# The smaller expert's gate in two products, with silu and product behind the turn and the fold

## Chip, cores and metric

One core of a Trainium2 chip runs the whole program: two transformer-like blocks in one launch. The metric is the device time of that core in microseconds (us), as the median of several runs. The engines are TensorE (PE; its weight loads are listed as PEld), VectorE (DVE), ScalarE (ACT), GpSimd (POOL) and SyncE (SP), which issues the weight transfers.

## What is computed

The first block ends in a mixture of experts, which takes about half the time. Eight experts, the two best for each of 256 tokens:

```python
def swiglu(h, w_gate, w_up, w_down):
    return (jax.nn.silu(h @ w_gate) * (h @ w_up)) @ w_down

def moe_swiglu(h, w_router, w_gate, w_up, w_down):
    ...
    for e in range(N_EXPERTS):
        y = swiglu(h, w_gate[e], w_up[e], w_down[e])
        out = out + gates[..., e:e + 1].astype(h.dtype) * y
    return out
```

The width of the model is 1024, an expert's hidden width is 3584, everything is float32.

## The kernel before

**Pairs of experts.** The experts are sorted by how many tokens they got and go in four pairs: expert i = 0 of a pair has 128 slots for tokens, the smaller one, i = 1, has 64. `experts` is written once for each engine (ACT from L1185, DVE from L1838, PE from L2719) and runs once for each pair.

**Weights come in pieces.** A piece is 128 partitions x 2048 float32. A pair has PC = 84 pieces. SP loads each into one of NRX = 6 raw slots (L692). ACT rounds it to fp32r, the high part `wh` (L1150), DVE takes the difference as the low part `wl` (L1729), each into one of NW = 4 slots. So ACT may take up piece c+4 when PE has used piece c (semaphore `moe_used`), and SP may load piece c+6 when DVE has split piece c (`lo_moe`).

**Products.** The tokens are split as well, into `xhl` (high and low). With 128 slots a product of full precision takes three matmuls for each 512 columns (`mm3`, L2251 to L2253): high by high, high by low, low by high. The smaller expert's high and low tokens, 64 and 64, fit side by side into one stationary operand (`BOTH`), so two matmuls do (`mm2`, L2257 and L2258); the rows 0 to 63 of the result and the rows 64 to 127 have then to be added. Its up product and its down product go so, its gate product doesn't: there both halves of the 128 columns hold the same 64 tokens, and `mm3` gives the whole gate on 128 partitions.

**The steps of a pair.** The hidden width goes in NEJ = 4 steps j of 1024, 1024, 1024 and 512 (`STEPS`); a full step has four pieces of gate, four of up and four of down for each expert, the last one two each. PE's order in a full step j = 1, 2 is: gate(0,j), up(0,j), down(1,j-1), turned(0,j), gate(1,j), up(1,j), down(0,j), turned(1,j). `porder` is the order of the pieces. Step 0 has no down(1,.), and `slots_turned` in it. The last step ends with last_down(0), turned(1,3), the gathering of the next pair's tokens (L2708), last_down(1) and the scattering (L2821, L2822); the latter lies inside the next pair's first gate.

**Between up and down.** ACT takes silu of the gate out of PSUM into `esg` (L1202), DVE multiplies it with up into `eact` (L1873). `turned` then turns `eact` into columns of hidden units, by transposes for expert 0 (L2779) and by a product with the matrix `fold`, which turns and adds the two halves, for expert 1 (L2781). ACT rounds the result (`actT_hi`, L1189), DVE takes the rest (`actT_lo`, L1844), and the down product reads both. ACT and DVE do all of this in the order of their own loop over the pieces; `turn_behind` says at which piece they come to the rounding of the turned activations.

Of the kernel before, what the change touches and what calls it, by code (L numbers as in the profile page):

```python
# [16 lines left out]
def build(nc, IN, out):  # L17
# [43 lines left out]
    with ctx:  # L61
# [410 lines left out]
        for j in range(NEJ):  # L472
            if j:
                turn_behind[ppos[1, "d", j - 1, LASTK[j - 1]]] = (0, j)
            turn_behind[ppos[0, "d", j, LASTK[j]]] = (1, j)
# [118 lines left out]

        def gate_bank(i, j):

            return (6 if j == 0 else 2) if i else 0
# [5 lines left out]
        y_hi = [[acth[:, 0, :], acth[:, 1, :]], [eactTh[:, 4 * (1 - half):4 * (2 - half), :].rearrange("p k s -> p (k s)") for half in range(2)]]  # L603
# [338 lines left out]
        def _(act):  # L942
# [242 lines left out]
            def experts(at, more_follow):  # L1185

                def actT_hi(i, j):
                    act.wait_ge(sg("moe_Tfull"), at(2 * NEJ, 2 * j + i + 1))
                    V.activation(eactTh[:, 0:STEPS[j][1] // P, 0:CAP[i]], turned_act(i, j),  # L1189
                                 ACT.Copy).then_inc(sg("moe_actTh"), 1)  # L1190
# [194 lines left out]
        def _(dve):  # L1385
# [452 lines left out]
            def experts(at, more_follow):  # L1838

                def actT_lo(i, j):  # L1840
                    ks = slice(0, STEPS[j][1] // P)
                    low = eactTh[:, ks, CAP[1]:P] if i else eactTl[:, ks, :]
                    dve.wait_ge(sg("moe_actTh"), at(2 * NEJ, 2 * j + i + 1))
                    V.tensor_tensor(low, turned_act(i, j), eactTh[:, ks, 0:CAP[i]].bitcast(F32),  # L1844
                                    ALU.subtract).then_inc(sg("moe_actTl"), 1)

# [20 lines left out]
                for c, (i, kind, j, k) in enumerate(porder[:-2]):  # L1867
                    tail = kind == "d" and j == NEJ - 1
                    if kind == "u" and k == LASTK[j]:
                        width = STEPS[j][1]  # L1870
                        dve.wait_ge(sg("moe_used"), at(PC, c + 1))
                        dve.wait_ge(sg("moe_silu"), at(2 * NEJ, 2 * j + i + 1))
                        V.tensor_tensor(eact[:, 0:width], esg[:, 0:width], wide(up_bank(i, j), width),  # L1873
                                        ALU.mult).then_inc(sg("moe_act"), 1)
                    if c in turn_behind:
                        actT_lo(*turn_behind[c])
                    if tail:
                        y_low(0, k)
                    weights_lo(c)
# [323 lines left out]
        def _(pe):  # L2203
# [515 lines left out]
            def experts(at, more_follow, first=False, opening=False):  # L2719
# [8 lines left out]
                def gate_up(i, b0, kind, j, between=None):  # L2728
# [4 lines left out]
                    for q in range(KD // rows):  # L2733
# [38 lines left out]
                def turned(i, j):  # L2772

                    pe.wait_ge(sg("moe_act"), at(2 * NEJ, 2 * j + i + 2))
                    to = turned_act(i, j)
                    for k in range(STEPS[j][1] // P):
                        rows = eact[:, k // 2 * 256:(k // 2 + 1) * 256].rearrange("p (m two) -> p two m", two=2)[:, k % 2, :]
                        if i == 0:
                            ins = T.transpose(to[:, k, :], rows, ident[:, :])  # L2779
                        else:  # L2780
                            ins = T.matmul(to[:, k, :], rows, fold[:, :], start=True, stop=True)  # L2781
                    ins.then_inc(sg("moe_Tfull"), 1)
# [21 lines left out]
                def last_down(i):  # L2804

                    parts_ready(i, NEJ - 1)
                    for half in range(2):
                        hs = slice(half * 512, (half + 1) * 512)
                        for part in range(2):
                            h_, l_ = here(i, "d", NEJ - 1, part, 2)  # L2810
                            for k in range(2):
                                ins = down_part(i, bank[4 + 2 * i + half], 2 * part + k, h_[:, k, hs], l_[:, k, hs],
                                                False, part == 1 and k == 1)
# [49 lines left out]
                last_down(0)  # L2863
                turned(1, NEJ - 1)
# [242 lines left out]
```

## Time and profile before

| | us |
|---|---|
| median of three runs | 1715.86 (1714.61 to 1716.14) |
| the profiled execution | 1716.64 |
| its span, first to last instruction | 1714.9 |

The profiled execution shows a matmul busy for 98% of the span, DVE for 80%, ACT for 65%, and DMA at 400 GB/s and more in the part of the experts, which lasts from about 451 to about 1346 us. The granted TensorE clock is 0.995 of full speed over the span, so nearly always the level of 2.4 GHz. A busy matmul row counts the time from a matmul's start to its modelled end, and these overlap; the distance from start to start tells what one costs. DVE's and ACT's rows don't overlap in this way: idle time between them is idle time, but for some 0.1 us at the end of each instruction.

### The profile page before, as it was taken

Reading aid. Unit: us, or ns where it says so; the run is one execution under the profiler, and the core shown is the slowest. Engines: PE = TensorE matmul, PEld = TensorE weight load, DVE = VectorE, ACT = ScalarE, POOL = GpSimd, SP = SyncE. Lnnn points to the kernel's source line nnn. Section 1 sums busy time; section 2 is a strip of 40 time slices with the busy share of each in tenths; the row PEclk is TensorE's granted clock in tenths of the full one; section 3 lists DMA queues with packets and bytes.
Section 4 is the critical chain, followed back from the end, with each engine's and each line's share of the span. In section 5 each row is a group of like instructions: output and inputs, shape, how many; then the busy total and the mean of one; then the engine's idle time right before and its main releaser. Section 6 shows DMA issues by size and latency. Waiting matters only on the chain.

```text
span 1714.9 us, 24639 instructions
## 1 busy us (share of the span) xinstructions
PE 1686.8 (98%) x9514; PEld 1461.7 (85%) x9514; DVE 1374.2 (80%) x1099; ACT 1118.0 (65%) x911; POOL 145.2 (8%) x152
## 2 busy tenths in 40 slices
PE   9999999999989999999999999999999899999999
PEld 8879999898878888888888888888888798889998
DVE  7576454746889998999998999989999789778775
ACT  6445343464557888777887788777877655855553
POOL 7200000000010200000000000000000018500000
PEclk9999999999999999999999999999999999999999
DMA  7455655553479999999999999999999654326551
GB/s 255 169 149 193 201 173 195 172 178 143 163 294 390 411 408 406 362 384 414 402 408 367 378 407 408 403 363 394 395 410 403 241 167 134 113 99 221 176 194 50
DMA packets 181300, 479.76 MB, mean 280 GB/s; under 512 B 11807, under 2 KB 80185, under 8 KB 166857
## 3 DMA queue, kind: packets, MB, share of 16 engines
q1 hardware_dynamic: 180185, 476.43, 74.5%
q10 hardware_dynamic: 1008, 1.84, 0.3%
q8 instruction: 76, 1.25, 0.3%
q14 instruction: 31, 0.25, 0.0%
HBM read 477.18 MB, written 1.05 MB: 279 GB/s over the span
## 4 chain that ended last, share of the span: by engine, by line
PE 74%; DVE 10%; issue 5%; ACT 4%; DMA 4%; POOL 2%; DVEq 0%; ACTq 0%; SPq 0%; POOLq 0%
PE bank L2251 19%; PE bank L2253 19%; PE bank L2252 19%; DVE wl L1729 6%; DMA arena<-in_moe_w_down 3%; ACT wh L1150 2%; PE bank L2257 2%; PE bank L2258 2%; PE bank L2781 1%; PE bank L2370 1%; PE bank L2378 1%; PE bank L2371 1%; POOL arena L925 1%; POOL arena L924 1%; DMA raw<-in_moe_w_down 1%
## 5 line engine op out<-in xcount | busy, mean ns | idle before, releaser
L1729 DVE TENSOR_TENSOR wl<-raw,wh 128x2048 fp32r<-128x2048 f32 x224 | 508.8, 2299 | 54.1 <-ACT wh L1150 53.3
L1150 ACT ACTIVATE wh<-raw 128x2048 fp32r<-128x2048 f32 x224 | 426.8, 1918 | 108.7 <-PE bank L2253 80.4
L2251 PE MATMUL bank<-wh,xhl 128*128 128x512 f32 x768 | 303.5, 395 | 4.5 <-issue 4.5
L452 DVE TENSOR_TENSOR wl<-raw,wh 128x2048 fp32r<-128x2048 f32 x112 | 254.8, 2292 | 64.8 <-ACT wh L445 63.0
L2253 PE MATMUL bank<-wh,xhl 128*128 128x512 f32 x768 | 299.9, 391 | 0.0
L2252 PE MATMUL bank<-wl,xhl 128*128 128x512 f32 x768 | 299.7, 390 | 0.0
L2251 PE MATMUL bank<-xhl,wh 128*128 128x256 f32 x944 | 268.0, 284 | 0.2 <-DVE wl L452 0.2
L2253 PE MATMUL bank<-xhl,wl 128*128 128x256 f32 x944 | 267.1, 283 | 0.0
L2252 PE MATMUL bank<-xhl,wh 128*128 128x256 f32 x944 | 267.1, 283 | 0.0
L1729 DVE TENSOR_TENSOR wl<-arena,wh 128x2048 fp32r<-128x2048 f32 x112 | 256.9, 2308 | 8.9 <-ACT wh L1150 8.1
L445 ACT ACTIVATE wh<-raw 128x2048 fp32r<-128x2048 f32 x116 | 219.3, 1912 | 33.1 <-PE bank L2253 19.5
L1150 ACT ACTIVATE wh<-arena 128x2048 fp32r<-128x2048 f32 x112 | 213.6, 1914 | 35.6 <-PE bank L2253 18.7
L2251 PEld LDWEIGHTS bank<-xhl,wh 128*128 128x128 f32 x944 | 181.1, 192 | 2.1 <-issue 0.9
L2252 PEld LDWEIGHTS bank<-xhl,wh 128*128 128x128 f32 x944 | 181.1, 192 | 0.8
L2253 PEld LDWEIGHTS bank<-xhl,wl 128*128 128x128 f32 x944 | 181.1, 192 | 0.0
L2251 PEld LDWEIGHTS bank<-wh,xhl 128*128 128x128 f32 x768 | 144.9, 189 | 34.0 <-issue 4.6
L2253 PEld LDWEIGHTS bank<-wh,xhl 128*128 128x128 f32 x768 | 144.6, 188 | 30.7
L2252 PEld LDWEIGHTS bank<-wl,xhl 128*128 128x128 f32 x768 | 144.8, 189 | 29.2
L2251 PE MATMUL bank<-wh,arena_r 128*128 128x512 f32 x224 | 88.9, 397 | 3.6 <-DVE wl L1729 3.1
L2257 PE MATMUL bank<-wh,xhl 128*128 128x512 f32 x224 | 88.4, 395 | 0.0
L2258 PE MATMUL bank<-wl,arena_r 128*128 128x512 f32 x224 | 88.0, 393 | 0.0
L2257 PE MATMUL bank<-wh,arena_r 128*128 128x512 f32 x224 | 87.9, 392 | 0.0
(485 smaller groups left out, 2459.4 us busy)
## 6 DMA issues: line engine op xcount, KB each, us to landing
raw<-in_moe_w_up SPq DMA_DIRECT2D x96, 1024.0 KB, 7.9
raw<-in_moe_w_gate SPq DMA_DIRECT2D x64, 1024.0 KB, 7.8
raw<-in_moe_w_down SPq DMA_DIRECT2D x64, 1024.0 KB, 8.2
arena<-in_moe_w_gate SPq DMA_DIRECT2D x48, 1024.0 KB, 7.8
arena<-in_moe_w_down SPq DMA_DIRECT2D x48, 1024.0 KB, 8.1
raw<-in_w_up SPq DMA_DIRECT2D x22, 1024.0 KB, 5.3
arena<-in_moe_w_up SPq DMA_DIRECT2D x16, 1024.0 KB, 10.4
raw<-in_gla_w_in SPq DMA_DIRECT2D x12, 1024.0 KB, 7.2
```

The lines of the kernel that those rows point to most:

```text
L445: nc.scalar.activation(wh[:, i % NW, :], raw[:, i % NR, :], ACT.Copy).then_inc(hi_ready[ph], 1)
L452: V.tensor_tensor(wl[:, i % NW, :], raw[:, i % NR, :], wh[:, i % NW, :].bitcast(F32), ALU.subtract).then_inc(lo_of[i][0], 1)
L924: G(V.tensor_scalar(m["mt"][:, k:S], bz[:, b, 0:S - k], col("b_conv", 4 * (3 - k) + b), None, ALU.mult))
L925: G(V.tensor_tensor(bc[:, b, k:S], bc[:, b, k:S], m["mt"][:, k:S], ALU.add), "b_pre")
L1150: V.activation(wh[:, s, :], src, ACT.Copy).then_inc(sg("hi_moe"), 1)
L1729: V.tensor_tensor(wl[:, s, :], moe_raw(c)[0], wh[:, s, :].bitcast(F32), ALU.subtract).then_inc(lo_moe, 1)
L2251: T.matmul(o, xh, yh, start=first, stop=False)
L2252: T.matmul(o, xh, yl, start=False, stop=False)
L2253: return T.matmul(o, xl, yh, start=False, stop=last)
L2257: T.matmul(o, x, yh, start=first, stop=False)
L2258: return T.matmul(o, x, yl, start=False, stop=last)
L2370: T.matmul(ps[:, :], xh[:, kk, ts], h_[:, k, :], start=(kk == 0), stop=False)
```

## The change

The gate product of expert 1 takes two matmuls for each 512 columns like its up. Its two halves can't go into silu before they are added, so the order behind it changes: ACT copies the gate out of PSUM to `esg` and later the up to `eact` (four counts of `moe_silu` a step instead of two), `turned(1, j)` waits for both copies and multiplies both with `fold`, 16 products in a full step instead of 8. ACT takes silu of the turned gate (`folded_silu`), DVE multiplies it with the turned up (`folded_act`) into `eact`, and `actT_hi` and `actT_lo` read that instead of PSUM. These work on 512 columns in a full step (256 in the last). The rounding of expert 1 moves one piece later in ACT's and DVE's loops. In the last step `turned(1, 3)` moves from behind last_down(0) to between its two halves, and that step's turned activations use the upper half of their tile. The diff, without the changes to the slices of `y_hi`:

```diff
-            turn_behind[ppos[0, "d", j, LASTK[j]]] = (1, j)
+            turn_behind[ppos[0, "d", j, LASTK[j] if j < NEJ - 1 else 0]] = (1, j)
...
+        def folded(j, up):
+            n = STEPS[j][1] // P * CAP[1]
+            return wide(6 if j == 0 else 2, 2 * n)[:, up * n:(up + 1) * n]
...
+        NSG = 4 * NEJ
+        def first_chunk(i, j):
+            return 4 if (i, j) == (1, NEJ - 1) else 0
...
                 def actT_hi(i, j):
...
+                    if i == 0:
+                        act.wait_ge(sg("moe_Tfull"), at(2 * NEJ, 2 * j + 1))
+                        src = turned_act(i, j)
+                    else:
+                        act.wait_ge(sg("moe_act"), at(2 * NEJ, 2 * j + 3))
+                        src = by_chunk(eact[:, 0:n * CAP[1]])
...
+                def folded_silu(j):
+                    g = folded(j, 0)
+                    act.wait_ge(sg("moe_Tfull"), at(2 * NEJ, 2 * j + 2))
+                    V.activation(esg[:, 0:g.shape[1]], g, ACT.Silu).then_inc(sg("moe_silu"), 1)
...
-                        V.activation(esg[:, 0:width], wide(gate_bank(i, j), width), ACT.Silu).then_inc(sg("moe_silu"), 1)
-                    if c in turn_behind:
-                        actT_hi(*turn_behind[c])
+                        V.activation(esg[:, 0:width], wide(gate_bank(i, j), width),
+                                     ACT.Copy if i else ACT.Silu).then_inc(sg("moe_silu"), 1)
+                    if kind == "u" and k == LASTK[j] and i == 1:
+                        width = STEPS[j][1]
+                        act.wait_ge(sg("moe_used"), at(PC, c + 1))
+                        V.activation(eact[:, 0:width], wide(up_bank(i, j), width), ACT.Copy).then_inc(sg("moe_silu"), 1)
+                    ready = turn_behind.get(c, (None, 0))
+                    if ready[0] == 0:
+                        actT_hi(*ready)
+                    if turn_behind.get(c - 1, (0, 0))[0] == 1:
+                        actT_hi(*turn_behind[c - 1])
...
+                    if ready[0] == 1:
+                        folded_silu(ready[1])
...
+                def folded_act(j):
+                    u = folded(j, 1)
+                    n = u.shape[1]
+                    dve.wait_ge(sg("moe_silu"), at(NSG, 4 * j + 4))
+                    V.tensor_tensor(eact[:, 0:n], esg[:, 0:n], u, ALU.mult).then_inc(sg("moe_act"), 1)
...
-                    if kind == "u" and k == LASTK[j]:
+                    if kind == "u" and k == LASTK[j] and i == 0:
...
-                                if kind == "u" and i == 1:
+                                if i == 1:
...
+                        pe.wait_ge(sg("moe_silu"), at(NSG, 4 * j + 3))
+                        for src, to in ((esg, by_chunk(folded(j, 0))), (eact, by_chunk(folded(j, 1)))):
+                            for k in range(n):
+                                ins = T.matmul(to[:, k, :], rows(src, k), fold[:, :], start=True, stop=True)
...
-                last_down(0)
-                turned(1, NEJ - 1)
+                last_down(0, lambda: turned(1, NEJ - 1))
```

DVE's loop changes as ACT's does: `folded_act` stands where `folded_silu` stands, and `actT_lo` of expert 1 one piece later.

## Rows read from the trace of the kernel before

**Rows 1.** The page, part 1: busy time and share of the span.
```profile
PE 1686.8 (98%) x9514; PEld 1461.7 (85%) x9514; DVE 1374.2 (80%) x1099; ACT 1118.0 (65%) x911; POOL 145.2 (8%) x152
```
**Rows 2.** Busy time by stretch: PE, PEld, DVE, ACT, POOL; clock, DMA share, GB/s.
```profile
723.32:947.60 224.28, 223.78 (x1042) 186.00 (x1041) 207.81 (x113) 176.67 (x115) 0.00 (x0) 1.00 1.00 394
750.10:912.90 162.80, 162.31 (x754) 134.57 (x753) 150.70 (x78) 132.33 (x87) 0.00 (x0) 1.00 1.02 404
```
**Rows 3.** The page, part 6: a piece's transfer, its size and time to landing.
```profile
raw<-in_moe_w_up SPq DMA_DIRECT2D x96, 1024.0 KB, 7.9
```
**Rows 4.** Who waited for whom, 723.32 to 947.60: total us, times, longest.
```profile
PE bank L2251 <- DVE wl L1729: 0.4, 2, 0.2
ACT wh L1150 <- PE bank L2253: 26.3, 33, 3.5
DVE wl L1729 <- ACT wh L1150: 15.4, 22, 3.0
```
**Rows 5.** Timeline of PE, steps 1 and 2 of the second pair: start, us, line.
```profile
761.35 0.39 PE L2257 MATMUL bank<-wh,arena_r 128*128 128x512 f32 x1
...
788.26 0.47 PE L2251 MATMUL bank<-wh,arena_r 128*128 128x512 f32 x1 [0.19 <-DVE wl L1729]
...
799.27 2.00 PE L2781 MATMUL bank<-fold,arena 128*128 128x64 f32 x16
801.08 0.48 PE L2251 MATMUL bank<-wh,xhl 128*128 128x512 f32 x1
...
801.85 0.39 PE L2251 MATMUL bank<-wh,xhl 128*128 128x512 f32 x1
...
802.53 0.39 PE L2251 MATMUL bank<-wh,xhl 128*128 128x512 f32 x1
```
**Rows 6.** Timeline of DVE in step 1 of that pair: six of its rows.
```profile
762.99 1.22 DVE L1873 TENSOR_TENSOR arena<-arena,bank 128x1024 f32<-128x1024 f32 x1
764.12 6.69 DVE L1729 TENSOR_TENSOR wl<-raw,wh 128x2048 fp32r<-128x2048 f32 x3
770.73 2.28 DVE L1729 TENSOR_TENSOR wl<-arena,wh 128x2048 fp32r<-128x2048 f32 x1
772.93 1.22 DVE L1844 TENSOR_TENSOR arena_r<-bank,arena_r 128x1024 fp32r<-128x1024 f32 x1
...
783.62 2.29 DVE L1729 TENSOR_TENSOR wl<-raw,wh 128x2048 fp32r<-128x2048 f32 x1 [0.67 <-ACT wh L1150]
785.83 4.49 DVE L1729 TENSOR_TENSOR wl<-arena,wh 128x2048 fp32r<-128x2048 f32 x2
```
**Rows 7.** Busy time by stretch: step 1, step 0 and step 3.
```profile
762.99:788.12 25.13, 25.09 (x114) 20.34 (x112) 24.46 (x14) 21.82 (x14) 0.00 (x0) 1.00 1.01 406
...
707.97:726.73 18.76, 18.76 (x94) 15.88 (x93) 16.72 (x13) 15.22 (x11) 0.00 (x0) 1.00 1.00 398
870.92:891.95 21.03, 21.03 (x95) 17.18 (x93) 21.03 (x11) 17.84 (x11) 0.00 (x0) 1.00 1.04 405
```
**Rows 8.** Timeline of PE: step 0 of that pair, then step 3.
```profile
706.33 0.39 PE L2251 MATMUL bank<-wh,xhl 128*128 128x512 f32 x1
...
726.73 0.39 PE L2251 MATMUL bank<-wh,arena_r 128*128 128x512 f32 x1
...
892.08 0.50 PE L2251 MATMUL bank<-wh,arena_r 128*128 128x512 f32 x1
...
896.31 1.05 PE L2781 MATMUL bank<-fold,arena 128*128 128x64 f32 x8
897.17 0.36 PE L2708 MATMUL bank<-arena_r,xnh 128*128 128x256 f32 x1
```
**Rows 9.** Timeline of ACT behind them: the copies of the gathered tokens.
```profile
898.25 4.03 ACT L1214 ACTIVATE xhl<-bank 128x512 fp32r<-128x512 f32 x8
```
**Rows 10.** The first pair: its step 0 on PE, and a stretch around it.
```profile
460.00:500.00 40.00, 35.52 (x174) 30.02 (x173) 31.49 (x29) 25.44 (x18) 5.86 (x3) 0.91 0.79 294
...
477.66 0.77 PE L2251 MATMUL bank<-wh,xhl 128*128 128x512 f32 x1 [4.47 <-issue]
```
**Rows 11.** Duration min/median/max in ns, of two groups: silu and rounding on ACT.
```profile
L1202 ACT ACTIVATE arena<-bank x32: 577/1029/1034, 459.3 to 1335.7; 128x1024 f32<-128x1024 f32 x24, 128x512 f32<-128x512 f32 x8
L1189 ACT ACTIVATE arena_r<-bank x32: 383/598/1031, 491.9 to 1345.9; 128x512 fp32r<-128x512 f32 x16, 128x1024 fp32r<-128x1024 f32 x12, 128x256 fp32r<-128x256 f32 x4
```

More of the change, by code:

```diff
@@ L601, in up_bank @@
             return (2 if j == 0 else 0) if i else 2
-        y_hi = [[acth[:, 0, :], acth[:, 1, :]], [eactTh[:, 4 * (1 - half):4 * (2 - half), :].rearrange("p k s -> p (k s)") for half in range(2)]]
+        y_hi = [[acth[:, 0, :], acth[:, 1, :]], [eactTh[:, 4 * half:4 * (half + 1), :].rearrange("p k s -> p (k s)") for half in range(2)]]
         y_lo = [[actl[:, 0, :], actl[:, 1, :]], [eactTl[:, 4 * half:4 * (half + 1), :].rearrange("p k s -> p (k s)") for half in range(2)]]
@@ L1840, in actT_lo @@
                 def actT_lo(i, j):
-                    ks = slice(0, STEPS[j][1] // P)
-                    low = eactTh[:, ks, CAP[1]:P] if i else eactTl[:, ks, :]
+                    n = STEPS[j][1] // P
+                    k0 = first_chunk(i, j)
+                    low = eactTh[:, k0:k0 + n, CAP[1]:P] if i else eactTl[:, 0:n, :]
+                    src = by_chunk(eact[:, 0:n * CAP[1]]) if i else turned_act(i, j)
                     dve.wait_ge(sg("moe_actTh"), at(2 * NEJ, 2 * j + i + 1))
-                    V.tensor_tensor(low, turned_act(i, j), eactTh[:, ks, 0:CAP[i]].bitcast(F32),
+                    V.tensor_tensor(low, src, eactTh[:, k0:k0 + n, 0:CAP[i]].bitcast(F32),
                                     ALU.subtract).then_inc(sg("moe_actTl"), 1)
+                def folded_act(j):
[3 more added lines that the diff above has]
+                    V.tensor_tensor(eact[:, 0:n], esg[:, 0:n], u, ALU.mult).then_inc(sg("moe_act"), 1)
                 def weights_lo(c):
@@ L2772, in turned, with rows @@
                 def turned(i, j):
[L2774 to L2781, printed above, removed]
+                    def rows(src, k):
+                        return src[:, k // 2 * 256:(k // 2 + 1) * 256].rearrange("p (m two) -> p two m", two=2)[:, k % 2, :]
+                    n = STEPS[j][1] // P
+                    if i == 0:
+                        pe.wait_ge(sg("moe_act"), at(2 * NEJ, 2 * j + 2))
+                        to = turned_act(i, j)
+                        for k in range(n):
+                            ins = T.transpose(to[:, k, :], rows(eact, k), ident[:, :])
+                    else:
+                        pe.wait_ge(sg("moe_silu"), at(NSG, 4 * j + 3))
+                        for src, to in ((esg, by_chunk(folded(j, 0))), (eact, by_chunk(folded(j, 1)))):
+                            for k in range(n):
+                                ins = T.matmul(to[:, k, :], rows(src, k), fold[:, :], start=True, stop=True)
                     ins.then_inc(sg("moe_Tfull"), 1)
@@ L2802, in down, with last_down @@
                         used(ins)
-                def last_down(i):
+                def last_down(i, between=None):
                     parts_ready(i, NEJ - 1)
                     for half in range(2):
+                        if half and between is not None:
+                            between()
                         hs = slice(half * 512, (half + 1) * 512)
@@ L2811, in last_down @@
                             for k in range(2):
-                                ins = down_part(i, bank[4 + 2 * i + half], 2 * part + k, h_[:, k, hs], l_[:, k, hs],
-                                                False, part == 1 and k == 1)
+                                ins = down_part(i, bank[4 + 2 * i + half], first_chunk(i, NEJ - 1) + 2 * part + k,
+                                                h_[:, k, hs], l_[:, k, hs], False, part == 1 and k == 1)
                             if half:
```

19 lines of the change are left out of this document (13 added, 6 removed).

## The prediction, made before the changed kernel was run

> **What bounds the kernel now.** I read the busy shares first. A matmul is busy for 98% of the span, DVE for 80% [rows 1], and in one whole pair of experts, 224.28 us long, PE is busy for 223.78 us and DVE for 207.81 us [rows 2]. That looks like a kernel bound by TensorE, from which every removed matmul comes off. The waits of the same pair say the same at first sight: PE waits for a split weight for 0.4 us in all, while ACT waits 26.3 us for PE to free a slot [rows 4].
>
> Next I read how the two engines run against each other inside a step. A matmul of 512 columns costs 0.227 us from start to start (801.85 to 802.53 for three) [rows 5]. So a piece that goes through three products holds PE for 12 x 0.227 = 2.72 us, and one that goes through two for 8 x 0.227 = 1.81 us. DVE takes 2.21 us for the split of a piece (three in 6.69 us, less the overlap at their ends: 764.12 to 770.73) [rows 6]. PE is therefore slower than DVE on three-product pieces and faster on two-product pieces. Only four split slots lie between them. In each full step there is a stretch that starts when up of expert 0 is done and ends at the start of down(0,j): down(1,j-1), the transposes, gate(1,j) and up(1,j). In step 1 it runs from 761.35 to 788.26, 26.91 us [rows 5], and ends with PE waiting 0.19 us for a split by DVE [rows 5]. Over that stretch, from the end of the last split that belongs to the slow part, DVE is busy for 24.46 of 25.13 us; its one gap is 0.67 us [rows 6, 7]. The reader is to see this: PE and DVE have the same length there, and PE only looks alone at the bound.
>
> Last the transfers. Between 750.1 and 912.9 the DMA share is 1.02 at 404 GB/s [rows 2]. A piece is 1024 KB, 1.049 MB [rows 3], so one lands every 2.59 us at that rate, and 84 need 218 us. The pair takes 224.3 us, so DMA alone would leave 6 us a pair.
>
> One rule of the Trainium skill speaks against this change. The page "Perfetto Trace Analysis", section "Identifying the Most-Contended Engine", says that matmul busy time is no measure of TensorE's headroom, that the busy share of its weight loads is to be used, and that the engine with the highest occupancy is to be optimized first. Here the weight loads are at 186.00 of 224.28 us, 83%, and DVE at 93% [rows 2]: by the rule DVE is the one to relieve, and the rows of the stretch agree. By the matmul row the sum would be the first rival's, by the rule about nothing is gained where DVE is full.
>
> **What is removed.** gate(1,j) loses one matmul of three. A pair has 7 blocks of 512 columns x 8 blocks of rows = 56 of them, 56 x 0.227 = 12.7 us of PE's time: 3.63 us in each full step, 1.82 us in the last. On DVE the product of 1024 columns (1.22 us [rows 6]) becomes one of 512, but it stood and stands outside the stretch.
>
> **What is added on PE.** A fold of a full step, 8 products (16 matmul rows), takes 1.81 us, from 799.27 to 801.08 [rows 5]; the last step's half takes 0.86 us, 896.31 to 897.17 [rows 8]. The change does twice as many: +1.81 us in each of three steps, +0.86 in the last, 6.3 us a pair. They lie in the slow part, where nothing else sets PE's pace, so they are paid in full. So PE's own work falls by 12.7 - 6.3 = 6.4 us a pair.
>
> **What the removed matmuls are worth, step by step.** Steps 1 and 2: the stretch can shrink only until DVE's chain is without a gap, since mult and rounding of expert 0 and the splits of all its pieces stay as they are. The gap is 0.67 us. With gate(1,j) at 1.81 us a piece PE will wait for splits several times in gate(1,j) and up(1,j), some 3 us in all. So -0.67 +1.81 = +1.14 us each. Step 0: the stretch is gate(1,0), transposes, slots, up(1,0), from 706.33 to 726.73 [rows 8]. DVE is busy in it for 16.72 of 18.76 us [rows 7], so it can shrink by 2.04 us; -2.04 +1.81 = -0.2 us. Step 3: DVE has no gap, 21.03 of 21.03 us [rows 7]; PE starts the second down piece at 892.08, right at the end of that chain [rows 8]. Nothing is gained, and the fold costs 0.86 us. That it stands between the halves now doesn't make it free: no split is late there that PE would otherwise wait for.
>
> **Copies and moved waits.** ACT gets copies of gate and up, 1.03 us each in a full step by silu's row [rows 11]. The gate's copy stands where silu stood. The up's copy is behind up(1,j), and turned(1,j), which waits for it, comes 10.9 us later in PE's order (four slow pieces), 2.7 us in the last step (one half of last_down). If that cover were gone it would cost 0.9 us a step; its place is then ahead of the split of piece c+4, which PE wants three pieces later. folded_silu and folded_act (512 columns, about 0.6 us by the rows of rounding at that size [rows 11]) hold the next split on ACT and DVE until PE has folded, as the rounding does today; the pause grows by 1.8 us. What waits behind it is the split of the next gate's fourth piece, which PE wants 8.2 us after the fold: I count it as hidden. At the end of the pair ACT's chain is longer by silu, and by the rounding, which is now behind one more split of 1.9 us. The copies of the gathered tokens start today 1.08 us behind PE's first gathering product (898.25 against 897.17) [rows 8, 9]. I add 0.3 us for them: between 0, if the earlier fold makes up for it, and 1.9 us, a whole split.
>
> **The sum.** Second and third pair: -0.2 + 2 x 1.14 + 0.86 + 0.3 = +3.2 us each. The first pair differs: its step 0 comes behind a pause of 4.47 us, and DVE is busy for only 31.49 of the 40 us around it [rows 10], so the whole 3.63 us and about 1 us of a wait behind it should come off: -4.6 + 1.8 + 2.3 + 1.2 = +0.7. In the last pair there is no gathering, but the scattering waits for low parts that stand behind the same chain; I take the same end: +3.2. Together +10.3 us, taken as +10: 1716.64 + 10 for an execution such as the profiled one, 1715.86 + 10 = **1725.9 us** for the median, which lies 0.8 us below the profiled time.
>
> Bounds of the unknown terms: if DVE's chain also loosens at its start, a stretch may win some 0.9 us more in each of the 8 middle steps and 1.6 us in each of three first ones (all of 3.63): -12 us. If none of the gaps can be used: 8 x 0.67 + 3 x 2.04 = +11 us, rarely all of it, and with the 1.9 us at the pairs' ends +6. That gives about 1714 to 1742 as outer ends and 1719 to 1733 as the forecast's own range.
>
> **Rivals.** *TensorE bound (faster).* PE's busy time is right, splits and transfers follow. Then 4 x 6.4 = 25.6 us come off: 1690. For it speaks that PE hardly waits in the whole pair [rows 4]; against it the 24.46 of 25.13 us [rows 7]. It decides if ACT and DVE can be 3 us ahead at the start of a stretch, for which there are only four slots. Chance 0.10. *Half of it.* The transfers allow 6 us a pair but DVE gives way in part, say by 3 us a pair: 1703. Chance 0.08. On what the transfers allow there is a page, "DMA: Bandwidth & Descriptors" of the Trainium skill, section "Bandwidth", which gives 425 GB/s for large transfers: by that a pair would need an estimated 207 us and not 218. The rows show 404 at a share above 1, and either figure leaves this rival open. *A draw.* Step 0 and the first pair give what steps 1 to 3 take: within 3.4 us of 1716. Chance 0.14. *The forecast*, slower by some 10 us by the full DVE chain: 0.56. *Transfers run dry (slower still).* The longer pause of DVE at the fold lets no raw slot free for about 6 us, the queue empties after step 0, and in the next stretch PE waits for data as well as for splits: at 2.59 us a piece a hole of one piece in two steps of each pair is 4 x 2 x 2.59 = 21 us, half of it on top of the forecast's waits: 1736. It decides if fewer than three transfers are under way at a fold; today a piece takes 7.9 us to land [rows 3], three pieces' time. Chance 0.12. That the change doesn't remove the matmuls is no rival: their number follows from the loops.
>
> **Numbers.** Faster by over 0.2%, which is about what a measurement of this kernel can tell from no change (3.4 us): 0.18. Within it: 0.14 and 0.03 from the near end of the forecast, 0.17. Slower: 0.53 + 0.12 = 0.65. The range that should hold 8 in 10 leaves out the first rival and parts of the second and of the last: 1707 to 1736.
>
> **What would show it.** Right: mm3 on xhl falls by 224 matmuls in each of three rows, mm2 grows by 224 in each of two, fold rows go from 224 to 448. In step 1 of the second pair the stretch to down(0,1) stays above 26 us with PE waiting some 3 us for DVE's splits, DVE has no gap in it, and two folds take 3.6 us; a pair takes about 227.5 us. PE's waits on DVE grow from 0.4 us to 7 or more a pair. Wrong: the pair is shorter than 224 us, or a stretch is shorter than 26 us (then the start of DVE's chain isn't where I put it), or ACT waits for transfers at each stretch's end (then the last rival).

## The result, and the profile after

The changed kernel takes 1728.6 us (median of 4, 1727.2 to 1729.7) against 1715.7 us (median of 4, 1714.6 to 1716.1): 1.0079 times the time before, 95% interval 1.0066 to 1.0091. It is slower by 13 us, where 10 us were forecast. The profiled execution has a span of 1726.9 us at a granted clock of 0.996.

First the page of the changed kernel, parts 1 and 5: busy time and share of the span; then a group's busy time, the mean ns of one, and the idle time ahead of it.

```profile
PE 1679.0 (97%) x9514; PEld 1440.9 (83%) x9514; DVE 1366.4 (79%) x1099; ACT 1135.7 (66%) x943; POOL 145.8 (8%) x152
...
L2300 PE MATMUL bank<-wh,xhl 128*128 128x512 f32 x544 | 214.4, 394 | 0.0
...
L2306 PE MATMUL bank<-wh,xhl 128*128 128x512 f32 x448 | 183.7, 410 | 18.8 <-DVE wl L1765 10.9
```

The change did what it says. The three-product rows went from 768 matmuls to 544, the two-product rows from 224 to 448. (The number of all PE instructions is the same by chance: 224 matmuls fewer, 112 folds of two records more.) PE is busy for 7.8 us less than in [rows 1], and the span is 12 us longer. The last row already says why: the two-product matmuls stood behind 18.8 us of idle time, 10.9 of them for splits by DVE.

Now three stretches of the second pair, to be held against [rows 2, 7]: a whole pair, step 1's stretch from down(1,0) to down(0,1), and step 0's stretch from gate(1,0) to down(0,0). They start at PE's first matmul of the stretch; those of [rows 7] start up to 1.6 us later in it. Columns: PE, PEld, DVE, ACT and POOL busy; clock, DMA share, GB/s.

```profile
726.88:954.78 227.90, 221.88 (x1041) 180.89 (x1040) 206.20 (x113) 181.19 (x122) 0.00 (x0) 1.00 0.99 387
764.51:791.04 26.53, 24.41 (x105) 18.40 (x104) 26.19 (x13) 22.39 (x13) 0.00 (x0) 1.00 1.01 391
709.92:727.26 17.34, 17.16 (x85) 14.00 (x84) 17.34 (x12) 16.89 (x11) 0.00 (x0) 1.00 1.01 414
```

In step 0's stretch DVE is busy for 17.34 of 17.34 us, and in step 1's for 26.19 of 26.53. With the same bounds DVE was busy for 26.24 of 26.91 us (step 1) and 18.36 of 20.40 (step 0) before. PE, which had 0.18 us of idle time in step 1's stretch before and none in step 0's, now has 2.12 and 0.18. The waits of that pair, to be held against [rows 4] (total us, times, longest):

```profile
ACT wh L1165 <- PE bank L2302: 19.3, 20, 3.5
...
PEld bank L2306 <- DVE wl L1765: 7.3, 10, 1.6
...
PE bank L2306 <- DVE wl L1765: 3.1, 5, 1.2
...
PE bank L2300 <- DVE wl L1765: 1.5, 5, 0.5
```

PE's weight loads of the two-product matmuls now wait 7.3 us a pair for DVE's splits, all its weight loads 9.0 us, where it was 1.3 before (the matmul of the piece waits on top of a load that waits, so the two rows overlap and aren't to be added). ACT waits less for PE, 19.3 us for 26.3.

The timeline of PE through step 1 of the second pair shows where (start, us, line; in brackets the idle time ahead and who ended it):

```profile
742.65 0.48 PE L2300 MATMUL bank<-wh,xhl 128*128 128x512 f32 x1
...
764.51 0.39 PE L2306 MATMUL bank<-wh,arena_r 128*128 128x512 f32 x1
...
779.56 0.50 PE L2306 MATMUL bank<-wh,xhl 128*128 128x512 f32 x1 [1.18 <-DVE wl L1765]
...
781.86 0.47 PE L2306 MATMUL bank<-wh,xhl 128*128 128x512 f32 x1 [0.17 <-DVE wl L1765]
...
788.65 0.50 PE L2306 MATMUL bank<-wh,xhl 128*128 128x512 f32 x1 [0.36 <-DVE wl L1765]
...
791.04 0.47 PE L2300 MATMUL bank<-wh,arena_r 128*128 128x512 f32 x1 [0.28 <-DVE wl L1765]
...
802.01 3.89 PE L2836 MATMUL bank<-fold,arena 128*128 128x64 f32 x32
805.71 0.48 PE L2300 MATMUL bank<-wh,xhl 128*128 128x512 f32 x1
```

The stretch is 791.04 - 764.51 = 26.53 us where it was 26.91: of the 3.63 us of removed matmuls 0.38 us are left. Behind it stands a fold of 805.71 - 802.01 = 3.70 us in place of 1.81. The step is 63.06 us, before 61.59.

The second pair piece by piece, each from the starts of PE's first and last matmul in the timeline:

| second pair | before, us | after, us | difference | forecast |
|---|---|---|---|---|
| step 0 (gate(0,0) second half, to gate(0,1)) | 49.48 | 49.05 | -0.43 | -0.2 |
| step 1 | 61.59 | 63.06 | +1.47 | +1.14 |
| step 2 | 61.59 | 62.70 | +1.11 | +1.14 |
| step 3, gathering, scattering | 51.48 | 53.09 | +1.61 | +1.16 |
| pair | 224.14 | 227.90 | +3.76 | +3.2 |

### The profile page after: what moved, and what is told of

Same layout as the page of the kernel before. It is cut to its first block, busy times and chain, and to the rows that moved or that the text cites. A ratio compares the mean times of both kernels' runs of the same rounds, so it can differ in the third digit from the quotient of the medians.

```text
span 1726.9 us, 24720 instructions
## 1 busy us (share of the span) xinstructions
PE 1679.0 (97%) x9514; PEld 1440.9 (83%) x9514; DVE 1366.4 (79%) x1099; ACT 1135.7 (66%) x943; POOL 145.8 (8%) x152
## 3 DMA queue, kind: packets, MB, share of 16 engines
HBM read 477.18 MB, written 1.05 MB: 277 GB/s over the span
## 4 chain that ended last, share of the span: by engine, by line
PE 66%; DVE 17%; issue 9%; ACT 4%; POOL 2%; DMA 1%; DVEq 0%; ACTq 0%; POOLq 0%; SPq 0%
PE bank L2300 17%; PE bank L2302 17%; PE bank L2301 17%; DVE wl L1765 11%; PE bank L2836 3%; ACT wh L1165 2%; DVE arena_r L1882 1%; PE bank L2419 1%; PE bank L2427 1%; PE bank L2420 1%; POOL arena L940 1%; POOL arena L939 1%; DMA arena<-in_moe_w_down 1%; DVE arena L1917 1%; PE bank L2306 1%
## 5 line engine op out<-in xcount | busy, mean ns | idle before, releaser
L1165 ACT ACTIVATE wh<-arena 128x2048 fp32r<-128x2048 f32 x112 | 214.1, 1915 | 38.8 <-PE bank L2302 19.9
L2300 PE MATMUL bank<-wh,xhl 128*128 128x512 f32 x544 | 214.4, 394 | 0.0
L2301 PE MATMUL bank<-wl,xhl 128*128 128x512 f32 x544 | 211.8, 389 | 0.0
L2302 PE MATMUL bank<-wh,xhl 128*128 128x512 f32 x544 | 211.8, 389 | 0.0
L2306 PE MATMUL bank<-wh,xhl 128*128 128x512 f32 x448 | 183.7, 410 | 18.8 <-DVE wl L1765 10.9
L2307 PE MATMUL bank<-wl,xhl 128*128 128x512 f32 x448 | 176.7, 394 | 0.0
L2301 PEld LDWEIGHTS bank<-wl,xhl 128*128 128x128 f32 x544 | 102.2, 188 | 20.4
L2307 PEld LDWEIGHTS bank<-wl,xhl 128*128 128x128 f32 x448 | 85.0, 190 | 16.0
```

Of the source, the lines that this page charges most:

```text
L1165: V.activation(wh[:, s, :], src, ACT.Copy).then_inc(sg("hi_moe"), 1)
L2300: T.matmul(o, xh, yh, start=first, stop=False)
L2301: T.matmul(o, xh, yl, start=False, stop=False)
L2302: return T.matmul(o, xl, yh, start=False, stop=last)
L2306: T.matmul(o, x, yh, start=first, stop=False)
L2307: return T.matmul(o, x, yl, start=False, stop=last)
```

## The experiments

The theory is that of the prediction: removed matmuls are worth only what DVE's chain in the stretch leaves (0.67 us in a full step, 2.04 in step 0), and the added folds are paid in full. The rivals are TensorE as the bound, the transfers running dry, and a loss that comes from the copies or the moved waits.

**One part alone: the two products without the rest.** e1 is the kernel before with this edit:

```
-    if kind == "u" and i == 1:
+    if i == 1:
         ins = mm2(b, x[:, kk, BOTH], h_[:, kk % rows, ns], l_[:, kk % rows, ns], kk == 0, kk == KD - 1)
```

> The kernel before, with the gate product of expert 1 in two matmuls and nothing else changed: the addition of its two halves ahead of silu is left out, so part of the computation is missing. It shows what the removed matmuls are worth by themselves. Theory (DVE's chain of splits ends the stretch from up(0,j) to down(0,j)): 0.7 us in each full step, 2 to 3 us in step 0, about 3.7 us a pair, 15 us in all: 1701. Rival, TensorE alone is the bound: 224 x 0.227 = 51 us, 1665. Rival, the transfers give the rest: 6 us a pair, 1691.

Measured: 1705.6 us (1704.5 to 1706.8), 0.9947 of before (0.9931 to 0.9962). Its busy time by stretch, down(1,0) to down(0,1), and PE's waits in it:

```profile
757.58:783.73 26.15, 24.34 (x106) 18.40 (x104) 26.15 (x14) 23.47 (x14) 0.00 (x0) 1.00 1.00 399
```
```profile
772.63 0.50 PE L2257 MATMUL bank<-wh,xhl 128*128 128x512 f32 x1 [1.19 <-DVE wl L1729]
774.92 0.47 PE L2257 MATMUL bank<-wh,xhl 128*128 128x512 f32 x1 [0.19 <-DVE wl L1729]
783.73 0.47 PE L2251 MATMUL bank<-wh,arena_r 128*128 128x512 f32 x1 [0.18 <-DVE wl L1729]
```

DVE is busy for the whole 26.15 us, and PE waits for it three times, the first time for the same 1.2 us as in the changed kernel. So copies and moved waits are not what makes PE wait: without any of them a full step wins 0.78 us (61.59 to 60.81) of 3.63. TensorE as the bound would have given 4 x 12.7 = 51 us for this edit; 9 came. That is less than the 15 expected. Step 0 and the full steps of the second pair came as expected (-2.23 and -0.78 us), but its step 3, where DVE had no gap, grew from 51.48 to 51.93 us, with waits of 0.37 and 0.70 us for splits in down(0,3), and step 0 of the first pair won 1.80 us.

**The added part alone: the folds twice.** e2 is the kernel before, and `turned(1, j)` does its folds a second time into a bank that nobody reads:

```
         else:
+            T.matmul(to[:, k, :], rows, fold[:, :], start=True, stop=True)
+    if i == 1:
+        n = STEPS[j][1] // P
+        to = bank[7 if j == 0 else 3][:, 0:n * CAP[1]].rearrange("p (k s) -> p k s", k=n)
+        for k in range(n):
+            rows = eact[:, k // 2 * 256:(k // 2 + 1) * 256].rearrange("p (m two) -> p two m", two=2)[:, k % 2, :]
             ins = T.matmul(to[:, k, :], rows, fold[:, :], start=True, stop=True)
```

> The kernel before, with each fold of expert 1 done a second time into a free bank: only the added products. Theory: they lie where PE alone sets the pace and are paid in full, 1.9 us in each full step and 0.9 us in the last, 6.6 us a pair, +26 us: 1742. Rival, they hide under a wait: 1716 to 1720. Together with the first run this should give the change: -15 + 26 = +11 us.

Measured: 1739.7 us (1738.4 to 1740.3), 1.0144 (1.0129 to 1.0160): +25.0 us, 6.2 us a pair. The second set of folds starts 1.83 us behind the first:

```profile
743.21 2.00 PE L2781 MATMUL bank<-fold,arena 128*128 128x64 f32 x16
...
745.04 2.06 PE L2787 MATMUL bank<-fold,arena 128*128 128x64 f32 x16
```

The folds are paid in full, four pairs times 6.3 us. e1 and e2 together give -9.1 + 25.0 = +15.9 us; the change as a whole gives +13. Each of the three differences is known to some 2 to 3 us, so the 3 us between them may be noise.

**The change in step 0 alone.** e5 makes every edit of the change conditional on (i, j) = (1, 0); steps 1 to 3 stay as before. The core of it:

```
-    if i == 1:
+    if i == 1 and (kind == "u" or j == 0):
         ins = mm2(...)
```

> The change in step 0 of each pair alone; steps 1 to 3 as before. In the trace of the changed kernel step 0 of the second pair is 0.4 us shorter than before, in the first pair it is as long as before. Theory: -0.4 us in three pairs, 1.2 us in all, 1714.5, not to be told from no change. Rival, TensorE bound: (3.63 - 1.89) x 4 = 7 us, 1709.

Measured: 1713.6 us (median of 11, 1711.2 to 1715.6), 0.9991 (0.9982 to 1.0000). In the second pair step 0 takes 739.11 - 690.06 = 49.05 us, the 0.43 us less of the table, and steps 1 and 2 take 61.59 and 61.56 us as before. Step 0 is a draw, and it lends nothing to or from its neighbours. The 13 us of loss are in steps 1 to 3.

**DVE relieved.** e3 (on the kernel before) and e4 (on the changed kernel) do half of the low parts of an expert's weights. What is left out: the other 1024 columns of each split keep what stood in the slot.

```
-    V.tensor_tensor(wl[:, s, :], moe_raw(c)[0], wh[:, s, :].bitcast(F32), ALU.subtract).then_inc(lo_moe, 1)
+    V.tensor_tensor(wl[:, s, 0:1024], moe_raw(c)[0][:, 0:1024], wh[:, s, 0:1024].bitcast(F32), ALU.subtract).then_inc(lo_moe, 1)
```

> The kernel before, with DVE taking the low part of only half the columns of each expert's piece (half of the low parts is left out): a split takes about 1.2 us instead of 2.3. Theory: PE hardly waits for DVE in the kernel before, so it gains only the 0.2 to 1 us waits at the stretches' ends, 1 us a pair: 1711, at most 6 us. Rival, DVE is the bound of the kernel before as a whole: more than 10 us.

> The changed kernel with the same relief of DVE (half of the low parts left out). Theory: PE no longer waits in the long stretch; a pair falls from 227.9 to about 218 us, where PE's own work (217 us) and the transfers (218 us) lie: 1728 - 38 = 1690, so that against the relieved kernel before the change gains some 20 us. Rival, the copies, the later rounding or the new waits are what costs: 1715 or more.

Measured: e3 1698.6 us (1697.6 to 1699.4), 0.9901 (0.9885 to 0.9918); e4 1696.8 us (1696.1 to 1698.3), 0.9892 (0.9876 to 0.9909). For e4 the rival (copies, rounding and new waits cost the time: 1715 or more) falls: with DVE relieved the changed kernel is 32 us shorter. But 38 us were expected, and a lead of some 20 us over the relieved kernel before; it is 1.7 us ahead of e3, where it was 13 us behind the kernel before. What holds e4 comes with the transfers, below. For e3 the expectation misses too. At most 6 us were expected of a kernel that I took to be limited by DVE almost nowhere; 16.5 us came. The busy time by stretch of e3, and the same up(1,1) as in [rows 5]:

```profile
716.00:938.00 222.00, 221.94 (x1040) 186.06 (x1039) 122.88 (x112) 175.98 (x114) 0.00 (x0) 1.00 1.01 397
```
```profile
769.12 0.39 PE L2257 MATMUL bank<-wh,xhl 128*128 128x512 f32 x1
...
776.38 0.39 PE L2251 MATMUL bank<-wh,arena_r 128*128 128x512 f32 x1
```

up(1,1) takes 7.26 us, as 32 x 0.227 must; before it took 7.78 (780.48 to 788.26), of which the trace calls 0.19 a wait on DVE. The whole step falls from 61.59 to 60.94 us. The larger part, 9.0 us, is at the first pair. PE reaches it 2.7 us earlier (458.57 to 455.88), and its step 0 falls from 55.95 to 49.62 us: 2.7 of that ahead of gate(1,0), where PE's pause shrinks from 4.47 to 1.79 us, 2.1 in the stretch and 1.5 in down(0,0) (a wait of 0.99 us among it). Not all of it is waiting: the 2.1 us in the stretch are the clock's, as PE's first matmuls of gate(1,0) show, before and then in e3 (the last columns: clock, DMA share, GB/s):

```profile
477.66:482.06 4.40, 4.40 (x10) 3.45 (x11) 1.19 (x2) 0.63 (x1) 0.00 (x0) 0.50 0.84 356
```
```profile
472.28:476.70 4.42, 4.42 (x19) 3.64 (x20) 1.19 (x2) 1.96 (x2) 0.00 (x0) 1.00 1.03 422
```

Behind the long pause the granted clock was 0.50, the level of 1.2 GHz, and 10 matmuls took the time in which e3, behind the short one, did 19 at 1.00: gate(1,0) took 13.07 us before and 11.01 in e3. So DVE cost the kernel before some 16 us, part of it through the clock behind PE's pauses. This matters for the one term of the sum that was badly sized (below).

The Trainium skill ("Perfetto Trace Analysis", section "Identifying the Most-Contended Engine") says to judge TensorE by its weight loads, and to optimize the engine with the highest occupancy first. The runs agree: weight loads are 186 of 224 us, DVE 208, and halving DVE's low parts gave 16.5 us where removing 12.7 us of matmuls a pair (e1) gave 9.

**Transfers.** e7 is the changed kernel with half of each piece transferred (the split reads the whole slot, and the other half of it is left from earlier), e8 is e4 with the same, e9 is e3 with the same:

```
-    sp.dma_start(to.rearrange("p (k n) -> p k n", k=src.shape[1]), src).then_inc(arrived, 16)
+    kh = src.shape[1] // 2
+    sp.dma_start(to.rearrange("p (k n) -> p k n", k=2 * kh)[:, 0:kh, :], src[:, 0:kh, :]).then_inc(arrived, 16)
```

> The changed kernel with half of each expert piece transferred (the other half of each raw slot is left as it was, so half of the weights is missing). Theory: DVE's chain still ends the stretches, so 0 to 4 us at the places where ACT waits for transfers today: 1724 to 1728. Rival, the transfers run dry: a fall to 1715 or below.

> The changed kernel with both, half the split and half the transfer (half of the weights and of their low parts left out). Theory: now PE's own work is the bound, about 217 to 218 us a pair, 4 x 6.1 us under the kernel before treated the same way, which should stand at about 1710: 1686. If ACT's chain (1.8 us a piece, 12 pieces and two more instructions in a long stretch) is next, up to 1 us a step more: 1694.

> The kernel before with half the split and half the transfer (half of the expert weights and of their low parts left out), to be set against the changed kernel treated the same way (1676.6). Theory: with DVE relieved PE never waited in the kernel before, so the transfers give nothing more: 1697 to 1699, and the change then gains about 22 us, near the 25 us that its matmuls and folds make on PE. Rival, the transfers held the relieved kernel before too: 1690 or below, and the change gains 10 us or less.

Measured: e7 1728.9 us, 1.0078 (1.0061 to 1.0094), the time of the changed kernel; e8 1676.6 us, 0.9774 (0.9758 to 0.9791); e9 1698.3 us, 0.9900 (0.9885 to 0.9915), the time of e3. The rival of transfers running dry falls with e7: half the bytes, and nothing comes back. But e8 is 20 us below e4, more than forecast. e4 and e8 by stretch, one pair each:

```profile
710.00:932.00 222.00, 219.28 (x1048) 183.24 (x1048) 122.86 (x116) 182.04 (x124) 0.00 (x0) 1.00 1.01 400
```
```profile
710.00:927.00 217.00, 216.42 (x1042) 182.60 (x1041) 121.61 (x113) 178.96 (x122) 0.00 (x0) 1.00 0.67 204
```

A pair of e4 takes 221.8 us (a third of the way from the first to the last of the four copies of the slots' table; before it is 225.0 by the same mark), and 84 pieces of 1.049 MB at its 400 GB/s take 220: behind DVE stand the transfers, some 3 us a pair below the time before. Once both are out of the way a pair takes 216.9 us, and PE is busy for 216.42 of 217. A full step is then 59.20 us against e9's and e3's 60.94: -1.74, which is -3.63 + 1.89. e8 minus e9 is -21.6 us. That is what the change is worth where TensorE is the bound, close to the first rival's 25.6. The rival's arithmetic was right, and its condition wasn't met.

On the DMA's limit the Trainium skill ("DMA: Bandwidth & Descriptors", section "Bandwidth") has 425 GB/s for a transfer of 16 MB, and 341 for one of 1 MB, the size of this kernel's pieces. By the first a pair would need an estimated 207 us and e4 would not have been held; the second is below what every trace here shows. The traces have 387 to 400 GB/s over whole pairs at a share of about 1.0 (394 before, so it is not 400 and more throughout, as "Time and profile before" has it), and up to 417 in a short stretch (e11, below); e4 was held, and the measurement decides.

**The fast pieces moved apart.** If DVE is late only because two-product pieces stand together, another order should help. e6 is the changed kernel with the pieces of a full step in another order (the list, PE's program and the waits alike):

```
-    g(0,j) u(0,j) d(1,j-1) t(0,j) g(1,j) u(1,j) d(0,j)
+    g(0,j) d(1,j-1) u(0,j) g(1,j) t(0,j) u(1,j) d(0,j)
```

> The changed kernel with another order of the pieces in steps 1 to 3: gate(0,j), down(1,j-1), up(0,j), gate(1,j), turned(0,j), up(1,j), down(0,j), turned(1,j). So never more than eight two-product pieces follow one another, as in step 0, where twelve did. PE's and DVE's work is the same. Theory (what costs is the length of the stretch, against four split slots): PE waits 3 us less in each full step, 220 to 221 us a pair against 227.9 us, near the 218 us that the transfers need: 1701, between 1695 and 1708. Rival, DVE or the transfers as a whole are the bound: no better than 1724.

Measured: 1725.2 us (1722.0 to 1728.9), 1.0063 (1.0046 to 1.0079). This misses by 24 us. A full step takes 62.06 us. The order brought a wait of its own, of PE for ACT's copy of the gate:

```profile
777.55 1.10 PE L2832 MATMUL bank<-ident,arena 128*128 128x128 f32 x8
779.94 0.50 PE L2307 MATMUL bank<-wh,xhl 128*128 128x512 f32 x1 [1.29 <-ACT arena L1229]
```

Since 24 pieces at 2.59 us are also 62.2 us, the transfers could be blamed. e12 is e6 with e7's edit, half of each piece transferred:

> The kernel with the fast pieces apart (1725.2 us), and of every piece of an expert's weights only the first half is transferred; the split reads the whole slot as before, and the second half of it is what an earlier transfer left there. Open is what holds its full steps at 62.06 us. Transfers' theory: PE's own work of such a step is 12 x 2.72 + 12 x 1.81 + 0.86 + 3.70 = 58.9 us, its waits for the gate's copy and for DVE add 1.7 us, 60.6; the rest to 62.06 (24 pieces at 2.59 us are 62.2) is the transfers'. With half of them a full step takes 60.6 us, a pair 4 to 5 us less, and the kernel about 1708. Rival: the transfers are only as long as the step is, as with the changed kernel (halving them there gave nothing, 1728.9 against 1728.6), and DVE and the copies set the step: 62 us a step, within 3 us of 1725.

Measured: 1722.2 us (1721.5 to 1723.0), 1.0037 (1.0025 to 1.0050). The transfers give 3 to 4 us, not 17; a full step still takes 62.08 us, although the wait for the gate's copy has fallen from 1.29 to 0.26 us. In its place PE waits 0.88 us for a split. Busy time by stretch, then DVE's timeline:

```profile
757.04:790.13 33.09, 31.68 (x139) 24.89 (x138) 33.09 (x17) 29.36 (x18) 0.00 (x0) 1.00 0.71 210
770.40:788.16 17.76, 16.44 (x73) 12.73 (x72) 17.76 (x10) 16.66 (x11) 0.00 (x0) 1.00 0.69 210
```
```profile
754.83 2.29 DVE L1767 TENSOR_TENSOR wl<-raw,wh 128x2048 fp32r<-128x2048 f32 x1 [1.33 <-ACT wh L1167]
757.04 4.49 DVE L1767 TENSOR_TENSOR wl<-arena,wh 128x2048 fp32r<-128x2048 f32 x2
761.45 8.89 DVE L1767 TENSOR_TENSOR wl<-raw,wh 128x2048 fp32r<-128x2048 f32 x4
770.25 2.29 DVE L1767 TENSOR_TENSOR wl<-arena,wh 128x2048 fp32r<-128x2048 f32 x1
```

DVE works without a gap through 33 us, and through the whole of gate(1,1) and up(1,1). Those eight fast pieces (14.5 us on PE) still stand together, against eight splits and now both the product and the rounding of expert 0 (8 x 2.21 + 2 x 1.13 = 19.9 us of DVE, from which only the lead that four slots allow can be taken off). Parting down(1,j-1) from them was the wrong cut; that wasn't tried further.

**The gate's fold moved into the stretch.** If a stretch is set by DVE, PE's work put into it should be free, and behind it it is paid. In the changed kernel both folds stand behind down(0,j). e10 does the gate's fold in the middle of up(1,j):

```
+    def folded_gate(j):
+        pe.wait_ge(sg("moe_silu"), at(NSG, 4 * j + 2))
+        for k in range(STEPS[j][1] // P):
+            T.matmul(by_chunk(folded(j, 0))[:, k, :], rows(esg, k), fold[:, :], start=True, stop=True)
...
-    gate_up(i, up_bank(i, j), "u", j)
+    gate_up(i, up_bank(i, j), "u", j, (lambda: folded_gate(j)) if i else None)
```

> The changed kernel with one move on TensorE: the 8 folds of the gate (4 in the last step) are issued in the middle of up(1,j), inside the stretch in which PE waits for DVE's splits anyway, and only the 8 folds of the up stay behind down(0,j). Theory: in a full step PE waits about 3 us there, so 1.9 us of folds vanish in the wait: full steps of 63.1 and 62.7 us become 61 us, step 0 gains about 0.8 us and step 3 about 0.6 us, a pair falls from 227.9 to 222.8 us, in all 1728 - 20 = 1708, below the kernel before. Rival, the folds delay the release of split slots and so DVE by their own length: 1724 or more. Rival, the transfers hold a full step at 62 us: 1721.

Measured: 1710.9 us (median of 8, 1709.1 to 1712.5), 0.9975 (0.9965 to 0.9986). Against the kernel before, step 0 of the second pair wins 1.77 us, full steps 0.1 us, and step 3 still loses 0.70. The moved fold isn't quite free: of its 1.85 us (half of 3.70) the full steps get back 1.57 and 1.18 us and step 0 gets back 1.34, and the stretch of step 1 grows from 26.53 to 26.94 us. So e11 does this in step 0 alone and leaves steps 1 to 3 as they were, which is e5 with e10's edit:

> The change in step 0 alone (steps 1 to 3 as in the kernel before), and in it the fold of the gate's copy stands in the middle of up(1,0), where PE runs at 1.81 us a piece and DVE sets the pace, and not beside the fold of the up's copy behind down(0,0). Theory (a product put into the stretch costs nothing as long as DVE is behind, one behind the stretch costs in full): moving the gate's fold took step 0 of the second pair from -0.43 us against the kernel before to -1.77 us when it was done in all four steps. The run with the change in step 0 alone took 1713.6 us; 4 x 1.34 us come off it: about 1708, 0.4% below the kernel before, and steps 1 and 2 of the second pair keep 61.6 us each. Rival (the 1.77 us of step 0 are lent by the next step: DVE is as late there and gives it back): no better than the run with the moved fold in all steps, about 1711, and step 1 of the second pair is above 62 us.

Measured: 1708.3 us (1706.7 to 1709.1), 0.9955 (0.9942 to 0.9969): faster than both kernels, by 7.7 us and by 20. Busy time of its step 0's stretch, then PE's timeline through step 0:

```profile
705.29:723.99 18.70, 18.70 (x102) 16.15 (x100) 18.41 (x14) 16.91 (x11) 0.00 (x0) 1.00 1.02 417
```
```profile
688.97 0.39 PE L2308 MATMUL bank<-wh,xhl 128*128 128x512 f32 x1
...
718.45 2.00 PE L2835 MATMUL bank<-fold,arena 128*128 128x64 f32 x16
720.26 0.48 PE L2314 MATMUL bank<-wh,xhl 128*128 128x512 f32 x1
...
723.99 0.39 PE L2308 MATMUL bank<-wh,arena_r 128*128 128x512 f32 x1
...
734.87 2.00 PE L2853 MATMUL bank<-fold,arena 128*128 128x64 f32 x16
736.68 0.48 PE L2308 MATMUL bank<-wh,xhl 128*128 128x512 f32 x1
```

The stretch is 18.70 us with the fold in it, where the changed kernel took 17.34 without and 1.89 more behind. PE has no wait in it, DVE is busy for 18.41: the two are level. Step 0 takes 736.68 - 688.97 = 47.71 us, 1.77 less than before, and the next two steps take 61.59 us each, so nothing is given back.

## Why the prediction was right, and where it wasn't

*The bound.* Right in kind. DVE's chain sets the stretches: e1 shows it full at 26.15 of 26.15 us, e4 and e8 show that the gain returns when DVE and transfers are out of the way. Too mild in size: "PE and DVE have the same length there" was put as a balance in which the kernel before loses 0.19 us a step, and e3 shows it losing 0.65 a step and 16 us in all. The transfers' 218 us a pair were near the mark as well: with DVE out of the way e4 was held at 221.8.

*The removed matmuls.* Full steps: the stretch was to shrink by 0.67 us; it shrank by 0.76 in e1, and by 0.38 and 0.77 in the changed kernel. Step 0 of the second pair: 2.04 forecast, 2.3 measured (20.40 us to 17.34, less 0.74 by which down(0,0) grew, a wait of 0.41 for a split among it). The waits of "some 3 us in all" were put too high: the four rows of step 1 come to 1.99 us. The rest of the 3.25 us that were not won went into lags between matmuls that no row calls a wait.

*The added folds.* 1.81 us forecast, 1.89 measured a full step; the second set of e2 starts 1.83 us behind the first.

*The copies, the moved waits.* The split behind the fold was counted as hidden, and it was: PE's next wait is 37 us behind the fold (742.65 to 779.56). Step 1 loses 0.33 us more than forecast, step 2 doesn't; e7, where step 1 takes 62.69 us, shows that these 0.36 us belong to the transfers. Step 3 with the gathering was sized at 1.16 and cost 1.61: the last fold 1.80 for 0.86, and the gathering behind it 4.70 for 4.27. These explain 1.37 of the 1.61; I take the 0.43 of the gathering for what 0.3 was set aside for, ACT's longer chain, which no run tested by itself. The trace agrees: ACT starts the copies of the gathered tokens 1.53 us behind PE's first gathering product (904.10), where it was 1.08, and PE waits for them:

```profile
905.63 4.00 ACT L1250 ACTIVATE xhl<-bank 128x512 fp32r<-128x512 f32 x8
```
```profile
906.27 0.50 PE L2757 MATMUL bank<-arena_r,xnh 128*128 128x256 f32 x2 [0.58 <-ACT xhl L1250]
```

*The first pair: the step that failed.* The sum had -4.6 + 1.8 = -2.8 us for its step 0, because DVE was "busy for only 31.49 of the 40 us around it". It gave nothing: 55.95 us before, 55.96 after. The pair came to +3.3 us instead of +0.7. The stretch, which was to lose all of its 3.63 us, lost 1.78 (22.65 to 20.87), the two folds cost 1.90 more than the one, and the wait of 1 us in down(0,0) that was to vanish stayed.

Where the 1.78 us come from can be read off DVE's rows between its first split of gate(1,0)'s weights and down(0,0), before and after. Before:

```profile
484.73 2.29 DVE L1729 TENSOR_TENSOR wl<-raw,wh 128x2048 fp32r<-128x2048 f32 x1 [5.19 <-ACT wh L1150]
487.50 5.01 DVE L1729 TENSOR_TENSOR wl<-raw,wh 128x2048 fp32r<-128x2048 f32 x2 [0.47 <-ACT wh L1150]
...
497.02 3.15 DVE L1729 TENSOR_TENSOR wl<-arena,wh 128x2048 fp32r<-128x2048 f32 x1
```

After, DVE, then GpSimd (POOL):

```profile
483.70 8.49 DVE L1765 TENSOR_TENSOR wl<-raw,wh 128x2048 fp32r<-128x2048 f32 x3 [3.91 <-ACT wh L1165]
...
495.45 3.17 DVE L1765 TENSOR_TENSOR wl<-arena,wh 128x2048 fp32r<-128x2048 f32 x1
```
```profile
484.07 2.87 POOL L906 TENSOR_TENSOR xn<-xn,arena 128x512 f32<-128x512 f32 x1 [52.94 <-PE bank L2307]
```

And the part from that split to down(0,0) after the change, by stretch and on PE:

```profile
483.70:498.77 15.07, 13.70 (x69) 11.00 (x68) 15.07 (x8) 14.40 (x11) 9.00 (x4) 1.00 0.70 244
```
```profile
498.77 0.48 PE L2300 MATMUL bank<-wh,arena_r 128*128 128x512 f32 x1 [1.05 <-DVE arena L1931]
...
502.77 0.50 PE L2300 MATMUL bank<-wh,arena_r 128*128 128x512 f32 x1 [1.00 <-DVE wl L1765]
```

The chain started 1.27 us sooner behind gate(1,0)'s start (5.80 us instead of 7.07), and it became 0.51 us shorter, 15.07 us instead of 15.58. It had gaps of 1.56 us (busy for 14.02 of 15.58), and they are all gone, but DVE's busy time in it grew by 1.05 us. The work is the same; the splits took longer. Three of them take 8.49 us here, and 6.69 in [rows 6], and GpSimd, which multiplies `xn` for the second block in this stretch, was busy for 9.00 us of it, 5.86 before. In both traces no split without a GpSimd instruction beside it took more than 2.30 us (326 before, 327 after); all longer ones, up to 3.39 us, had one. So two things were misread: a busy share over 40 us was taken for slack of the chain, and DVE's work in the chain was taken to be of fixed length, while it grew beside GpSimd as the idle time went. No run took GpSimd's work out, so the second is read from the traces and not tested.

*The last pair* was to cost as much as the others, +3.2. It cost about +1.5: from the start of its gate(0,0) the kernels are 10.55 us apart, and at their ends 12.0. Its step 0 won 0.91 us (49.43 to 48.52), steps 1 and 2 cost 1.12 and 1.16 as forecast, and all that stands behind them cost 0.12 in place of 1.16; why the end hides the folds was not tested. The two misses are +2.6 and -1.7, pairs 2 and 3 add 0.6 and 0.0; together 11.8 of the 12.0 us of the spans, for 10.3 of the sum. That the sum came near is in part luck.

*The rivals.* TensorE as the bound: refuted by e1; its price is confirmed by e8 - e9 = -21.6 us. Half of it: refuted by e1, DVE gives way by 0.1 us. A draw: true of step 0 alone (e5). Transfers run dry: refuted by e7. PE's waits for splits grew to 3.1 + 1.5 = 4.6 us a pair by the matmul rows, by which the 0.4 us before were read, so the "7 or more" was too high; by the rows of the weight loads they grew from 1.3 to 9.0.

## What to carry to other kernels

When a kernel alternates stretches where one engine is slower with stretches where the other is, and only a few slots lie between them, cost an edit by the stretch it stands in: here work removed where PE waits for DVE was worth DVE's gap there (0.67 us forecast, 0.76 in e1), and work added where PE sets the pace cost its full length (1.89 us). So trade the other way round: put the added work (here the gate's fold) into the stretch where the engine waits, and make the exchange only in the steps where the other engine has room; of the same edits one placement gave +13 us and another -7.7. And read slack from the gaps in the chain itself, not from a busy share over a window around it, and ask whether its instructions will keep their length: here splits grew from 2.3 us to up to 3.4 beside GpSimd.

## What the runs showed that was not expected

- A wait that the trace shows as 0.19 us cost 0.52: up(1,1) took 7.78 us before and 7.26 when DVE was relieved, with no other wait in the matmul rows. Of the rest the rows show only a weight load that waits 0.31 us for a split (785.97); short lags behind a late split lengthen a run of matmuls without a matmul row that says so.
- Behind PE's pause of 4.47 us in the first pair the granted clock was 0.50 for the first 4.4 us of gate(1,0), the lower of the two levels of 1.2 and 2.4 GHz, and 1.00 after. Matmuls there start 0.43 us apart (478.65 to 479.07 in the kernel before), not 0.227. With DVE relieved (e3) the pause was 1.79 us and the clock 1.00 throughout, worth 2.06 us.
- Splits on DVE took 2.28 to 2.30 us alone and up to 3.39 with GpSimd at work beside them; one and the same GpSimd instruction took 1.09 us in e4 and 2.87 in the changed kernel.
- Two full loads side by side, DVE busy for 206.20 of a pair's 227.90 us and DMA at a share of 0.99, hid one another in the changed kernel: with only the transfers halved nothing moved (e7), with only DVE halved 32 us did (e4), and with both 52 (e8).
